# Two convolved gate stages change from plain products to seven block products, and the halves of accumulators share PSUM banks

## The reference

```python
def swiglu_ffn(h, w_gu, w_down):      # first block, twice (gu0/down0, gu1/down1)
    gate, up = split(h @ w_gu)
    return (silu(gate) * up) @ w_down

def conv_ffn(h, w_gate, w_up, conv_w, conv_b, w_down):   # second block, twice
    g = causal_dwconv(h @ w_gate, conv_w, conv_b)        # 3 taps along the tokens
    return (jax.nn.silu(g) * (h @ w_up)) @ w_down
```

## Time and profile before

| | us |
|---|---|
| median of 3 runs | 2436.04 (2434.38 to 2436.42) |
| profiled execution, its own time | 2434.37 |
| profiled execution, span | 2432.7 |
| TensorE (PE) busy | 2384.4 (98%) |
| VectorE (DVE) busy | 1438.4 (59%) |
| ScalarE (ACT) busy | 939.8 (39%) |
| GpSimd (POOL) busy | 320.0 (13%) |

### The profile page before, as it was taken

One profiled execution on the slowest core, in us unless ns is written; L12 is line 12 of the kernel. 1 busy time (PEld: TensorE's weight loads), 2 busy tenths in 40 slices (PEclk: granted clock), 3 DMA queues, 4 the chain that ended last, 5 costly groups with the idle time before them and its releaser, 6 DMA issues.

```text
span 2432.7 us, 34459 instructions
## 1 busy us (share of the span) xinstructions
PE 2384.4 (98%) x13747; PEld 2013.6 (83%) x13747; DVE 1438.4 (59%) x1948; ACT 939.8 (39%) x1191; POOL 320.0 (13%) x258
## 2 busy tenths in 40 slices
PE   7699999999999999999999999999999999999999
PEld 7688899988886789998878679888888878888887
DVE  8845877845437678776774746444434545544532
ACT  5422544623226534445233644232222444322322
POOL 6403000002003240000232031000121002000000
PEclk9899999999999999999999999999999999999999
DMA  2433333333232133323333112322332312323232
GB/s 57 98 98 99 92 105 105 94 95 111 93 96 59 38 104 95 106 79 107 95 108 105 53 35 87 104 88 92 88 107 78 104 53 70 102 89 104 72 100 89
DMA packets 291257, 216.02 MB, mean 89 GB/s; under 512 B 9460, under 2 KB 281994, under 8 KB 291050
## 3 DMA queue, kind: packets, MB, share of 16 engines
q1 hardware_dynamic: 285370, 207.14, 28.4%
q0 software_dynamic: 2384, 5.80, 1.0%
q10 hardware_dynamic: 3360, 1.02, 0.2%
HBM read 205.28 MB, written 2.10 MB: 85 GB/s over the span
## 4 chain that ended last, share of the span: by engine, by line
PE 91%; DVE 5%; ACT 2%; issue 1%; SPq 1%; ACTq 0%; DMA 0%; POOL 0%; DVEq 0%
PE psum L1068 11%; PE psum L1070 11%; PE psum L1069 11%; PE psum L1281 6%; PE psum L1283 6%; PE psum L1282 6%; PE psum L1313 5%; PE psum L1314 5%; PE psum L1312 5%; PE psum L1454 2%; PE psum L1456 2%; PE psum L1455 2%; PE psum L1180 1%; PE psum L1176 1%; DVE w_lo L2877 1%
## 5 line engine op out<-in xcount | busy, mean ns | idle before, releaser
L2004 ACT CAST w_hi<-w_stage 128x2048 fp32r<-128x2048 f32 x165 | 315.6, 1913 | 932.0 <-PE psum L1070 482.2
L2877 DVE TENSOR_TENSOR w_lo<-w_stage,w_hi 128x2048 fp32r<-128x2048 f32 x162 | 381.1, 2352 | 447.4 <-ACT w_hi L2004 447.4
L1068 PE MATMUL psum<-x_hi,w_hi 128*128 128x512 f32 x536 | 209.0, 390 | 0.0
L1069 PE MATMUL psum<-x_lo,w_hi 128*128 128x512 f32 x536 | 208.6, 389 | 0.0
L1070 PE MATMUL psum<-x_hi,w_lo 128*128 128x512 f32 x536 | 208.5, 389 | 0.0
L1281 PE MATMUL psum<-x_hi,w_hi 128*128 128x512 f32 x512 | 200.1, 391 | 0.0
L1282 PE MATMUL psum<-x_lo,w_hi 128*128 128x512 f32 x512 | 199.3, 389 | 0.0
L1283 PE MATMUL psum<-x_hi,w_lo 128*128 128x512 f32 x512 | 199.2, 389 | 0.0
L2968 DVE TENSOR_TENSOR w_lo<-w_parts,w_hi 128x1024 fp32r<-128x1024 f32 x108 | 131.8, 1223 | 63.5 <-ACT w_hi L2062 60.4
L1313 PE MATMUL psum<-x_sum_lo,w_hi 128*128 128x256 f32 x576 | 163.0, 283 | 0.0
L1314 PE MATMUL psum<-x_sum_hi,w_lo 128*128 128x256 f32 x576 | 163.0, 283 | 0.0
(11 more groups left out here) (576 smaller groups left out, 5573.1 us busy)
## 6 DMA issues: line engine op xcount, KB each, us to landing
w_stage<-in_ffn_w_down_dram SPq DMA_DIRECT2D x64, 704.0 KB, 4.5
w_parts<-in_ffn_w_gu_dram SPq DMA_DIRECT2D x144, 256.0 KB, 3.4
w_stage<-in_ffn_w_gate_dram SPq DMA_DIRECT2D x22, 1024.0 KB, 5.3
w_stage<-in_ffn_w_up_dram SPq DMA_DIRECT2D x22, 1024.0 KB, 5.3
w_stage<-in_sb_w_qkv_dram SPq DMA_DIRECT2D x12, 1024.0 KB, 5.0
w_stage<-in_od_w_in_dram SPq DMA_DIRECT2D x12, 1024.0 KB, 5.3
w_stage<-in_ev_w_in_dram SPq DMA_DIRECT2D x10, 1024.0 KB, 5.1
w_stage<-in_ssm_w_glu_dram SPq DMA_DIRECT2D x8, 1024.0 KB, 5.6
```

Of the source, the lines that this page charges most:

```text
L1068: nc.tensor.matmul(dst, hi, x_hi, start=(start and k == 0), stop=False)
L1069: nc.tensor.matmul(dst, hi, x_lo, start=False, stop=False)
L2004: nc.scalar.copy(whi[:, half, :], wst[:, half, :]).then_inc(whi_done, 1)
L2877: V.tensor_tensor(wlo[:, half, :], wst[:, half, :], whi[:, half, :].bitcast(F32), ALU.subtract).then_inc(wlo_done, 1)
```

## The change

`conv0` and `conv1` now run three plain iterations and eight seven-product iterations each, in place of eleven plain ones. `gu0` and `gu1` keep two and nine. For the convolved stages the sums of x are made by twelve passes from the high and low parts of x, in two portions between plain iterations, each pass waiting for the one before. VectorE's order in a convolved iteration is written out anew (`conv_iteration`). In all four stages y and w now share a bank (its two halves, banks 0 and 1), z lies in banks 2 and 3, and x has two banks per tile, used in turn; the last sum goes into the upper half of x's bank, so that one Silu and one product cover the full width where two half-width ones did. `seed` waits for one more product than before. SP waits for product 9 instead of 7 before it loads the first down weights. The down stages after the convolved stages take the hidden chunks as they arrive, as those after `gu0` and `gu1` do. The core of the diff:

```diff
-SEVEN = ("gu0", "gu1")
-PLAIN = 2
-SEVEN_ITERS = FC // 2 - PLAIN
+SEVEN = {"gu0": 2, "gu1": 2, "conv0": 3, "conv1": 3}
+SEVEN_ITERS = {name: FC // 2 - plain for name, plain in SEVEN.items()}
+X_STEPS = {"gu0": 4, "gu1": 4, "conv0": 12, "conv1": 12}
...
-        y_bank, w_bank, x_bank, z_bank = ([bank[n] for n in pair] for pair in ((0, 2), (1, 3), (4, 6), (5, 7)))
+        def y_half(tile):
+            return bank[tile][:, 0:HALF]
+        def w_half(tile):
+            return bank[tile][:, HALF:SEQ]
+        def z_half(tile):
+            return bank[2 + tile][:, 0:HALF]
+        def x_bank(tile, i):
+            return bank[4 + 2 * tile + i % 2]
...
# SP
-                sp.wait_ge(product_done, products_count(name, SEVEN_ITERS - 1, 7))
+                sp.wait_ge(product_done, products_count(name, SEVEN_ITERS[name] - 1, 9))
...
# TensorE
                         if i > 0:
                             pe.wait_ge(copied, copied_count(name, i - 1, 2 * tile + 1))
-                        product(z_bank[tile], i, 2 * tile, *t1, True)
-                        if i > 0 and tile == 0:
-                            pe.wait_ge(act_out, gated_count(name, i - 1, 3))
-                        if i > 0 and tile == 1:
-                            pe.wait_ge(evac_done, hidden_count(name, i - 1, 3))
-                        product(x_bank[tile], i, 2 * tile + 1, *b11, True)
+                        else:
+                            pe.wait_ge(evac_done, hidden_count(name, 0, tile - 1))
+                        product(z_half(tile), i, 2 * tile, *t1, True)
+                        if i > 1:
+                            pe.wait_ge(evac_done, hidden_count(name, i - 2, 2))
+                        product(x_of[tile], i, 2 * tile + 1, *b11, True)
...
# ScalarE, start of a stage
+                for i in range(plain - 1):
+                    split(st.it0 + i + 1, 0, st.part0 + i * 4 + 2)
+                    plain_gates(i)
+                    split(st.it0 + i + 1, 1, st.part0 + i * 4 + 4)
+                for n, made in ((2, 3), (3, 7), (0, 10), (1, 12)) if conv else ((0, 1), (2, 2), (1, 3), (3, 4)):
+                    round_sum(n, made)
+                plain_gates(plain - 1)
+                for n, tile in ((0, 0), (0, 1), (1, 0), (1, 1)):
+                    round_pair(0, n, tile)
...
# VectorE
                 def seed(i, tile):
-                    dve.wait_ge(product_done, products_count(name, i, 5 + 2 * tile))
+                    dve.wait_ge(product_done, products_count(name, i, 6 + 2 * tile))
...
+                def x_sums_from_parts_early():      # 7 passes of 128x1024, each waits for the one before
+                def x_sums_from_parts_late():       # 5 more, after both splits of the last plain iteration
...
+                def conv_start():
+                    plain_iteration(0)
+                    x_sums_from_parts_early()
+                    plain_iteration(1)
+                    x_sums_from_parts_late()
+                    for n, count in ((2, 1), (3, 2), (0, 3), (1, 4)):
+                        x_sum_low(n, count)
+                    for tile in range(2):
+                        sums_of_two(0, tile)
+                    for u in range(2):
+                        taps(4 + u, u, bank[u])
+                    low_pair(0, 0, 0)
+                    for tile in range(2):
+                        sum_of_three(0, tile)
+                    plain_hidden(2, 0)
+                    low_pair(0, 0, 1)
+                    plain_hidden(2, 1)
+                    for tile in range(2):
+                        sum_of_four(0, tile)
+                    low_pair(0, 1, 0)
+
+                def conv_iteration(i):
+                    if i > 0:
+                        taps_second(i - 1)
+                    low_pair(i, 1, 1)
+                    if i > 0:
+                        hidden_first(i - 1)
+                        hidden_second(i - 1)
+                    low_pair(i, 2, 0)
+                    sums_of_two(i + 1, 0)
+                    low_pair(i, 2, 1)
+                    seed(i, 0)
+                    low_last(i, 0)
+                    low_last(i, 1)
+                    seed(i, 1)
+                    sums_of_two(i + 1, 1)
+                    sum_of_three(i + 1, 0)
+                    sum_of_three(i + 1, 1)
+                    join(i, 0)
+                    low_pair(i + 1, 0, 0)
+                    sum_of_four(i + 1, 0)
+                    sum_of_four(i + 1, 1)
+                    join(i, 1)
+                    low_pair(i + 1, 0, 1)
+                    taps_first(i)
+                    low_pair(i + 1, 1, 0)
...
# last iteration, ScalarE: next_split(0), then the second gate, two casts of hidden chunks,
# (conv: the second Silu), next_split(1), nine casts. VectorE: next_split(0), (conv: two taps),
# the second product and two low parts, next_split(1), nine low parts.
```

More of the change, by code:

```diff
@@ L520, in a12_count, with a22_slot, ring_half_used @@
         def a12_count(name, i):
-            return (SEVEN.index(name) * SEVEN_ITERS + i + 1) * 32
-        def a22_slot(i):
-            return A22 + i % 2
+            return (before(name) + i + 1) * 32
+        def a22_slot(name, i):
+            return A22 + (i + SEVEN_ITERS[name] + 1) % 2
         def ring_slot(i, n):
             return (i * PRODUCTS + n) % RING
+        def ring_half_used(name, half):
+            end = SEVEN_ITERS[name] - 1
+            return products_count(name, end, 1 + max(n for n in range(PRODUCTS) if ring_slot(end, n) // (RING // 2) == half))
@@ L1324, in seven_products @@
                 pe.wait_ge(low_ready, rounded_count(name, 0, 0))
-                for i in range(SEVEN_ITERS):
+                for i in range(SEVEN_ITERS[name]):
+                    x_of = [x_bank(tile, i)[:, 0:HALF] for tile in range(2)]
                     for tile in range(2):
@@ L2034, in seven_gate_stage @@
                 st = ST[name]
-                end = SEVEN_ITERS - 1
+                plain, end = SEVEN[name], SEVEN_ITERS[name] - 1
+                conv = name in ("conv0", "conv1")
+                layer = int(name[-1])
                 def plain_gates(i):
@@ L2051, in ring_free @@
                     else:
[L2052 removed]
+                        act.wait_ge(part_done, st.part0 + (plain - 1) * 4 + (2 if last <= -4 else 4))
                 def round_pair(i, n, tile):
@@ new lines, in fork, with gate_first @@
+                    if tile == 1 and i > 0:
+                        act.wait_ge(evac_done, hidden_count(name, i - 1, 1))
+                    nc.scalar.copy(y_half(tile), x_bank(tile, i)[:, 0:HALF]).then_inc(copied, 1)
+                def gate_first(i):
+                    m = 2 * (plain + i)
+                    act.wait_ge(product_done, products_count(name, i, 10))
+                    act.wait_ge(evac_done, hidden_count(name, i, -1))
+                    if conv:
+                        nc.scalar.activation(tmp_a[:, 0, :], bank[0], ACT.Identity, bias=tap(layer, TAPS, m),
+                                             scale=tap(layer, TAPS - 1, m)).then_inc(conv_a, 1)
+                    else:
+                        nc.scalar.activation(tmp_a[:, 0, :], bank[0], ACT.Silu).then_inc(act_out, 1)
@@ L2986, in join, with taps_first @@
                     dve.wait_ge(product_done, products_count(name, i, 9 + 2 * tile))
-                    if tile == 0 and i > 0:
-                        dve.wait_ge(act_out, gated_count(name, i - 1, 2))
-                    V.tensor_tensor(joined[:, tile, :], x_bank[tile][:, 0:HALF], z_kept[:, tile, :], ALU.add).then_inc(added, 1)
+                    V.tensor_tensor(x[:, HALF:SEQ], x[:, 0:HALF], z_kept[:, tile, :], ALU.add).then_inc(added, 1)
+                def taps_first(i):
+                    taps(2 * (plain + i), 0, bank[0])
@@ L3038, in seven_gate_stage, with plain_iteration, start @@
-                for i in range(SEVEN_ITERS):
+                def plain_iteration(i):
+                    split(st.it0 + i + 1, 0)
+                    if conv:
+                        for u in range(2):
+                            taps(i * 2 + u, u, bank[u])
+                    for u in range(2):
+                        plain_hidden(i, u)
+                    split(st.it0 + i + 1, 1)
+                def start():
+                    plain_iteration(0)
+                    x_sums()
+                    for tile in range(2):
+                        sums_of_two(0, tile)
+                    for n, count in ((0, 1), (2, 2), (1, 3), (3, 4)):
+                        x_sum_low(n, count)
+                    for tile in range(2):
+                        sum_of_three(0, tile)
+                    for tile in range(2):
+                        low_pair(0, 0, tile)
+                    for tile in range(2):
+                        sum_of_four(0, tile)
+                    for u in range(2):
+                        plain_hidden(1, u)
+                    low_pair(0, 1, 0)
@@ L3078, in residual @@
+                if conv:
```

(8 more changed lines are left out.)

433 lines of the change are left out of this document (221 added, 212 removed).

## The result

| | before | after |
|---|---|---|
| median of 5 runs each, us | 2434.69 (2434.14 to 2436.42) | 2450.39 (2447.27 to 2451.31) |
| profiled execution, span, us | 2432.7 | 2448.6 |
| PE busy | 2384.4 | 2371.0 |
| DVE busy | 1438.4 | 1603.1 |
| ACT busy | 939.8 | 1044.6 |

The changed kernel is **slower**: the ratio is 1.0059, with a 95% interval of 1.0044 to 1.0074. The prediction was 2438, with a range of 2429 to 2446, and the time lies above the range.

What follows compares the result with a forecast made beforehand. The prediction took the chain of waits, 91% TensorE, as the bound. Terms -25.6 + 7.9 + 5.8 + 7.5 + 6.6 gave +2.2 us, 2436.5 for the profiled execution; median forecast 2438, range 2429 to 2446.

Steps and rivals of the forecast that it cites:

- Fewer matmuls: Convolved stages: eight iterations in each of two go from 21.763 to 20.16 us if nothing stalls, -25.6 us.
- Steady iterations: Convolved and gu stages: VectorE's and ScalarE's extra work stays under TensorE's 20.16 us period, cost 0.
- Starts: Start of conv0 and conv1: TensorE stands 3.95 us each while VectorE finishes extra sums before product 1, +7.9 us.
- gu ends: Ends of gu0 and gu1: down-weight load waits for product 9, not 7, and 2.88 us shows twice, +5.8 us.
- Convolved ends: Ends of conv0 and conv1: late load, cast and low part stop TensorE 3.75 us each, +7.5 us.
- Clock: TensorE after six stops of 3.6 to 3.8 us: four falls to the lower clock at 1.65 us each, +6.6 us.
- its rival: TensorE's clock holds through the stops: change of -4.3 to -2.7, 2431.7 to 2433.3 us; chance 0.13.
- The one on the slow side: Clock falls after every stop and at some stays down a second stretch: 2441.5 to 2446 us; chance 0.20.
- VectorE as the bound: Convolved iterations: VectorE half a microsecond late in 16 iterations, +8 on the forecast, 2446 us; chance 0.07.
- stops that stay away: Stage ends: load lands sooner or is covered, only the starts remain, 2421.6 up to 2424 us; chance 0.10.

Runs made afterwards that it cites:

- kernel with four edits: Changed kernel with VectorE's start reordered, down load half by half, TensorE not waiting for the last Silu, first down cast and low part before the last taps; 2409.21 us.
- VectorE's new order alone: Changed kernel with the sums product 1 needs made between the second iteration's plain hidden chunks, ahead of the late x sums; 2439.4 us.

## Why the prediction was wrong

- **Fewer matmuls, -25.6.** Right: 20.16 us per iteration without idle, and 12.8 us per stage in the kernel with four edits.
- **Steady iterations, 0.** Right. VectorE was busy 18.39 of 20.16 us where I had worked out 19.0, ScalarE 11.38.
- **Starts, +7.9.** Right in place, releaser and size: 2 x 3.66 = 7.3, released by VectorE's product (L2975). The times that I wrote down give 3.85 us each (1541.6 less 1537.75) and not the 3.95 that went into the sum, so 0.2 of the 0.6 is a slip.
- **gu ends, +5.8.** Right in mechanism, short in size: +7.6. I let two products of delay, 2.88 us, show in full and took the landing as it was. From issue to ScalarE's cast it was 7.64 us in gu0 before and 7.28 in gu1, which I did not look at; in the changed kernel it was 8.02 and 8.61 there and 8.32 and 8.77 at the convolved ends, and in two of the experiments up to 9.5 and 9.7. A transfer that ends a chain should have had bounds.
- **Convolved ends, +7.5.** This is the step that failed: they cost 13.6. I wrote that "queued behind the late cast on ScalarE are the last Silu and eleven casts of hidden chunks", and then asked only when those chunks were needed. I had not asked who waits for the Silu. TensorE does, in the first line of the down stage, ahead of a product that doesn't read it. So the late load was followed by a cast, a low part, two taps and a Silu, not by a cast and a low part. The entry without the Silu took 2.2 and 1.4 us off, and putting that wait back into the fastest kernel cost 12.7. By the changed kernel's own rows the Silu comes 2.2 us after the low part (1724.37 against 1722.17), and the rest of the miss, 0.7 and 1.1 us, is the landing.
- **Clock, +6.6.** The mechanism is right and the size was off: six falls instead of four, and 6.8 us of low clock instead of 3.3 at each of the four ends, 11.1 us. I gave the row with an idle of 3.64 and a clock of 1.00 as much weight as the one at 95.83, which resembled my stops more. That 1.00 was misread as well. The trace of the kernel before holds no clock record before 24.8 us, and the column prints 1.00 where there is none. A window and one line of TensorE, the same work before and after that moment:

```profile
20.00:24.00 4.00, 4.00 (x20) 3.81 (x19) 3.90 (x9) 3.53 (x7) 3.84 (x4) 1.00 0.00 0
```
```profile
23.15 1.06 PE L939 MATMUL psum<-ident,bl_own 128*128 128x128 f32 x4
...
27.43 0.60 PE L939 MATMUL psum<-ident,bl_own 128*128 128x128 f32 x4
```

Four matmuls take 1.06 us and then 0.60, and the starts of the pairs at L936 and L937 lie 0.43 us apart from 20.16 on and 0.22 from 25.87 on. So TensorE ran at the lower level until about there under a printed 1.00, and the row at 9.30 says nothing for a clock that holds, in the forecast or in its rival. The Trainium skill, "TensorE: Matmul & The Clock Gate", section "What's actually happening", has the lower clock as the state that a pause brings back: the runs agree for all ten stops of over 3.6 us in the changed kernel and in the one with the load at product 7, and this rule should have had the larger chance.
- **The rivals.** The one on the slow side (0.20) described what the clock did, but with the ends as short as in the forecast it stopped at 2446. It was its stops that were too short. VectorE as the bound did not come. Neither did stops that stay away.

The misses add up by the terms: -0.6 at the starts, +1.8 at the gu ends, +6.1 at the convolved ends, +4.5 of clock, +0.3 in the last two down stages, +0.5 at the start of gu0 and gu1 and +1.0 of start-up are 13.6 of the 13.7 us between a forecast change of 2.2 and the measured 15.9 of span.

## What to carry to other kernels

When a load or a pass becomes late, list not only what is queued behind it but every wait of another engine on each thing in that list, down to the engine that sets the end; here a wait for all gates, in front of a product that doesn't need the last of them, cost 12.7 us in the fastest kernel. Price a stop on TensorE with the slow stretch behind it: here that was 1.3 to 2.5 us on top of each of the six. And a change whose steady part is right can lose at its borders more than it gains, so try the borders one at a time before giving it up: four small edits turned +15.7 us into -26. And before a clock printed as 1.00 counts as evidence, compare the distances of the same matmuls in another stretch.

## What the hardware showed that I had not expected

The low-clock stretch at the borders lasted 3.4, 6.8 or, after stops of 6.71 and 8.00 us (the convolved ends with VectorE's new order alone), 10.2 us. The length of the stop alone did not fix it: 7.04 us at the end of conv1 in the changed kernel was followed by 6.8, and the same stop of 3.66 us at the starts of conv0 and conv1 was followed by 6.8 and 3.4 us in the kernel with the load at product 7, and by 3.4 and 3.4 in the changed one. At the borders studied here, stops of 0.5 to 1.42 us kept the clock in all runs, those of 1.98 to 2.00 lost it in three of four, and those of 3.6 and longer in all where nothing filled the stop. Away from the borders it is less simple: in the kernel with the load at product 7 the clock also fell for 3.4 us at 1394.8, in an attention stage, behind idle stretches of 0.65 and 0.74 us, where the kernel before went through the same work at 1.00. And where the cast waited for the load, the time from the issue of this load to the cast spread from 7.3 us (gu1's end in the kernel before) to 9.7 (conv1's end with VectorE's new order). No run varies what else moves then, so the cause of the spread stays open.
